# The last down unit of a mixture of experts, loaded and finished by column halves

## The chip, the cores and the metric

The kernel runs on one core of a Trainium2 chip. A time is the device time of one execution in microseconds (us), and the figure that counts is the median of several runs. A core has TensorE (matrix products; its weight loads are listed apart as PEld), VectorE (DVE), ScalarE (ACT), GpSimd (POOL) and SyncE (SP, which here only issues DMAs). Each engine works through its own queue in order; semaphores order the engines against each other. Numbers are 32-bit floats throughout.

## The reference

One layer of a decoder for 256 prompt rows and 32 sample rows of width 1024. Attention comes first and is not touched here. After it:

```python
logits = hx @ w_router + b_router            # 32 experts
top_val, top_idx = top_k(logits, 4)
comb = sum(one_hot(top_idx) * softmax(top_val))
for each expert e:
    gu   = hx @ w_gate_up[e] + b_gate_up[e]  # 1024 -> 2048
    gate = minimum(gu[:, 0::2], 7); up = clip(gu[:, 1::2], -7, 7)
    act  = gate * sigmoid(1.702 * gate) * (up + 1)
    acc += comb[:, e] * (act @ w_down[e] + b_down[e])   # 1024 -> 1024
out = layer_norm(alpha * hx + acc, ln2_g, ln2_b)
```

The weights of the 32 experts are 403 MB in all and are read once.

## The kernel before

The experts go in 16 pairs. Each expert computes only the rows that were routed to it: up to 64 rows in a first pass, gathered by products with a 0/1 matrix (`pick`). The two experts of a pair share TensorE: each product has 64 columns of the array, expert 0 in the upper and expert 1 in the lower 64 rows of the result. There are further passes for experts with more than 64 rows; they were not taken here (`further_passes` takes its `otherwise` branch).

The weights of a pair arrive in 12 units of 2 MB, in a ring of 9 slots of 16 KB a partition: units 0 to 7 are gate and up weights, units 8 to 11 down weights. SyncE issues all loads, in order, each as soon as its slot is free. The last pair has a routine of its own, `load_last_pair`. Its unit 11 comes in two loads of 1 MB, one for each of two contraction chunks `c`, each with its semaphore (`half_in[8 + c]`). When the gate and up products are done, SyncE loads the layer norm's gains and biases (`load_last`, semaphore `ln2_in`), behind the weights in the same queue.

On TensorE the end of the last pair is `last_down` and `mix_last`. `last_down` computes `y = act @ w_down` into two banks of 512 columns: bank 4 has the lower column half of `y`, bank 5 the upper. It runs over units `v` (8 to 11), chunks `c`, column halves and experts. Between, `keep_sums` copies the running sums of earlier pairs from `acc` into banks 0 to 3 and 7, by products with the identity, so that the last combine can add to them there: bank 2t + half has prompt tile `t`, and bank 7 the 32 sample rows, of which each quarter of 256 columns sits on 32 partitions (`mix_samples`, four products on 32 columns of the array each).

When both banks are done (`down_done`), ScalarE copies bank 4 to `ybuf` and VectorE copies bank 5 (`take_lower`, `take_upper`). `mix_last` waits for both and multiplies `ybuf` by `spread`, which holds the routing weights and puts the rows back in their places: tile 0, its two halves; the samples; tile 1, its two halves.

VectorE then takes the second layer norm. It first waits for `ln2_in`, and takes statistics from the banks (`y_statistics`, one `bn_stats` for each half, then `bn_aggr`): tile 0, the samples, tile 1. ScalarE takes the roots (`root_y`) and centres tile 0 out of the banks; VectorE multiplies tile 0 by the gain (GpSimd adds its bias), and does samples and tile 1 by itself. SyncE stores the pieces. A matrix product with a mean matrix (bank 6) joins the statistics of the four sample quarters.

Every product on 32-bit data appears in the trace as two passes, so that eight products of the source are sixteen in the trace.

Of the kernel before, what the change touches and what calls it, by code (L numbers as in the profile page):

```python
# [109 lines left out]
def build_layer(nc, x_prompt, x_sample, cache_k, cache_v, state_k, state_v, page_table, w_in, gn_moba,  # L110
# [9 lines left out]
    def place(name, shape, at=None, dt=F32):  # L120
# [89 lines left out]
    names = """ident_in consts_in x_in0 x_in1 x_in2 pages_in w_in_landed0 w_in_landed1 w_in_landed2 wout_in0 wout_in1  # L210
        wout_in2 wout_in3 k_landed0 k_landed1 k_landed2 k_landed3 v_landed0 v_landed1 v_landed2 v_landed3 ln1_in
        router_in bdn_in ln2_in x_turned xT_even xT_odd projected proj_copied kv_turned vtok_ready kstage_ready
# [12 lines left out]
        y_ready mixed added y_varied y_rooted y_scaled y_centred y_gained y_normed y_done y_moments y_shared  # L225
        sums_whole copies_out
        results_out dve_done dve_moe pass_added""".split()
# [4 lines left out]
    w_landed = [sems[f"w_in_landed{i}"] for i in range(3)]  # L232
    wout_in = [sems[f"wout_in{i}"] for i in range(4)]
    k_landed = [sems[f"k_landed{i}"] for i in range(KRING)]
# [167 lines left out]
    def _(sp):  # L402
# [107 lines left out]
        def load_last_pair():  # L510

            p, m = PAIRS - 1, PAIRS // PERIOD
            for u in range(8):
                unit_free(m, 0, u, WHOLE)
                dst = ring[slot_of(0, u)][:, :].rearrange("p (e k n) -> p e k n", e=2, k=2)
                k, c = 256 * (u % 4), slice(D * (u // 4), D * (u // 4) + D)
                for e in range(2):
                    sp.dma_start(dst[:, e], w_gate_up[0, 2 * p + e, k:k + 256, c].rearrange(
                        "(p k) n -> p k n", p=128)).then_inc(half_in[u], 16)
                sp.sem_inc(unit_in[slot_of(0, u)], 16)  # L520
            for u in range(8, UNITS - 1):
                unit_free(m, 0, u, WHOLE if u < RING else LATE)
                load_unit(p, 0, u)
            unit_free(m, 0, UNITS - 1, LATE)
            dst = ring[slot_of(0, UNITS - 1)][:, :].rearrange("p (e c n) -> p e c n", e=2, c=2)
            src = w_down[0, pair_of(p), 512:1024, :].rearrange("e (p c) n -> p e c n", c=4)
            for c in range(2):
                sp.dma_start(dst[:, :, c, :], src[:, :, 2 + c, :]).then_inc(half_in[8 + c], 16)
            sp.sem_inc(unit_in[slot_of(0, UNITS - 1)], 16)
# [205 lines left out]
    def _(pe):  # L735
# [341 lines left out]

        pe.wait_ge(wout_in[2], 16)
        pe.wait_ge(wout_in[3], 16)
        pe.wait_ge(S.outT_ready, 3)  # L1080
# [157 lines left out]

        def mix_samples(out, start):

            for q in range(4):
                ins = nc.tensor.matmul(out[NS * q:NS * q + NS, 0:256], spread[:, SEQ:T],
                                       ybuf[:, 256 * q:256 * q + 256], start=start, stop=True,
                                       tile_position=(0, NS * q))
            return ins
# [114 lines left out]
        def last_down():  # L1360
# [3 lines left out]
            keep_sums(2, 0)  # L1364
            for v in range(4):
                w = ring[slot_of(0, 8 + v)]
                if v < 3:
                    pe.wait_ge(unit_in[slot_of(0, 8 + v)], unit_value(last // PERIOD, 0, 8 + v))
                pe.wait_ge(S.actT_ready, last * 2 + (1 if v < 2 else 2))
                for c in range(2):  # L1370
                    j = 2 * v + c
                    if v == 3:
                        pe.wait_ge(half_in[8 + c], 16)
                    for half in range(2):
                        for e in range(2):
                            at = 2048 * e + 1024 * c + 512 * half
                            ins = nc.tensor.matmul(bank[4 + half][64 * e:64 * e + 64, :], actT[:, j, 64 * e:64 * e + 64],
                                                   w[:, at:at + 512], start=(j == 0), stop=(j == KC - 1))
                if v < 3:
                    ins.then_inc(S.unit_used, 1)  # L1380
                if v == 0:
                    turn_act(last, 2 * last + 2, (1,))
                    keep_sums(1, 0)
                if v == 1:
                    keep_sums(1, 1)
            ins.then_inc(S.down_done, 1)

# [7 lines left out]

        def mix_last():

            pe.wait_ge(S.y_ready, last * 2 + 2)
            for j in (0, 1, 4, 2, 3):
                t, half = divmod(j, 2)  # L1400
                if t == 2:
                    ins = mix_samples(bank[7], False)
                else:
                    ins = nc.tensor.matmul(bank[j][:, :], spread[:, 128 * t:128 * t + 128],
                                           ybuf[:, 512 * half:512 * half + 512], start=False, stop=True)
                ins.then_inc(S.mixed, 1)

        last_gate_up({1: lambda: combine(last - 1), 5: turn_first, 6: keep_first})
        last_down()
        mix_last()  # L1410

# [31 lines left out]
    def _(act):  # L1443
# [221 lines left out]

        def take_lower():
            act.wait_ge(S.down_done, PAIRS)
            copy(ybuf[:, 0:512], bank[4][:, :]).then_inc(S.y_ready, 1)

        nc.scalar.activation(s_(c_junk), s_(c_junk), ACT.Sqrt)  # L1670
        further_passes(act, more, none, first=take_lower, otherwise=take_lower)

# [15 lines left out]
    def _(dve):  # L1688
# [478 lines left out]

        def take_upper():
            dve.wait_ge(S.down_done, PAIRS)
            V.tensor_copy(ybuf[:, 512:1024], bank[5][:, :]).then_inc(S.y_ready, 1)  # L2170

        def sums_to_sbuf():
            take_upper()
            for n, j in enumerate((0, 1, 4, 2, 3)):
                t, half = divmod(j, 2)
# [7 lines left out]

        further_passes(dve, more, none, sums_to_sbuf, sums_kept, take_upper)
        dve.wait_ge(S.ln2_in, 160)
        mv = [s_(c_mv + 4 * t, 4) for t in range(3)]

        def y_statistics(t, after):
            for half in range(2):
                dve.wait_ge(S.mixed, 5 * last + after + half)  # L2190
                step.on(V.bn_stats(s_(c_stat + 12 * t + 6 * half, 6), bank[2 * t + half][:, :]))
            dve.wait_ge(step.sem, step.n)
            link(V.bn_aggr(mv[t][:, 0:2], s_(c_stat + 12 * t, 12).rearrange("p (a c) -> p a c", a=2)))
            V.tensor_scalar(mv[t][:, 1:2], mv[t][:, 1:2], LN_EPS, None, ALU.add).then_inc(S.y_varied, 1)

        y_statistics(0, 1)
        dve.wait_ge(S.mixed, 5 * last + 3)
        link(V.bn_stats(s_(c_stat + 24, 6), bank[7][:, 0:256]))
# [6 lines left out]
                               ALU.mult).then_inc(S.y_scaled, 1)  # L2205
        y_statistics(1, 4)
        dve.wait_ge(S.y_shared, 1)
# [4 lines left out]
        link(V.reciprocal(mv[1][:, 1:2], mv[1][:, 1:2]))  # L2212

        for half in range(2):
            c = slice(512 * half, 512 * half + 512)
# [42 lines left out]
```

## Time and profile before

| | us |
|---|---|
| median of three runs | 1143.01 |
| lowest, highest | 1141.0, 1143.07 |
| profiled execution, span from first to last instruction | 1138.4 |
| median less span (what lies around it) | 4.6 |
| TensorE busy in the span | 1100.8 |
| mean rate of all DMAs | 399 GB/s |

The profiled execution's time is its span, which leaves out what lies ahead of the first and behind the last instruction. The last gate and up products of the last pair end just before 1104 us, and the rest of the span holds what is described here. The granted clock of TensorE was 1.00 in all stretches between 1100 and 1130. DMA engines were at or over 0.99 busy until 1118 us and 0.53 in the us from 1120.

In rows, `PE` and `PEld` are TensorE's products and weight loads, `SPq` is SyncE issuing a DMA, and the bracket at a row's end is the idle time of the engine before it with what released it. Ends of TensorE's products are modelled.

### The profile page before, as it was taken

How to read it: one execution, taken by the hardware profiler on the slowest of the kernel's cores; microseconds unless marked ns; L12 is line 12 of the kernel's file. 1: busy time of each engine (PE TensorE's matmuls, PEld its weight loads, DVE VectorE, ACT ScalarE, POOL GpSimd, SP SyncE). 2: the span in 40 equal slices, each digit the busy share in tenths (PEclk: the TensorE clock that was granted, in tenths of full speed). 3: DMA queues.
4: the chain of work that ended last, by engine and by line, in shares of the span. 5: the costliest groups of instructions: out<-in, count | busy, mean ns of one | idle time of the engine just before them, and what ended most of it. 6: DMA issues, size and time to landing. Idle time of an engine off the chain costs nothing.

```text
span 1138.4 us, 14132 instructions
## 1 busy us (share of the span) xinstructions
PE 1100.8 (97%) x5468; PEld 462.9 (41%) x5469; DVE 293.2 (26%) x734; ACT 204.1 (18%) x481; POOL 30.2 (3%) x65
## 2 busy tenths in 40 slices
PE   8999999999999999999999999999999999999996
PEld 6876764433333333333333333333333333333331
DVE  1553757530303030212121212121202031303123
ACT  2322412411111120202020202020201111111112
POOL 0110111000000000000000000000000000000001
PEclk9999999999999999999999999999999999999998
DMA  9967778999999999999999999999999999999994
GB/s 361 347 221 247 286 274 344 418 431 408 429 420 425 432 431 430 430 430 431 432 429 431 432 431 432 431 431 431 431 431 432 432 431 431 431 430 430 397 423 192
DMA packets 61348, 454.37 MB, mean 399 GB/s; under 512 B 6595, under 2 KB 19539, under 8 KB 35572
## 3 DMA queue, kind: packets, MB, share of 16 engines
q1 hardware_dynamic: 58818, 440.97, 93.0%
q0 software_dynamic: 1728, 10.75, 2.5%
q10 hardware_dynamic: 754, 1.98, 0.4%
q8 instruction: 34, 0.56, 0.2%
q14 instruction: 14, 0.11, 0.0%
HBM read 450.14 MB, written 11.93 MB: 406 GB/s over the span
## 4 chain that ended last, share of the span: by engine, by line
PE 79%; DMA 16%; ACT 2%; DVE 1%; SPq 1%; issue 1%; DVEq 0%
PE bank L1176 26%; PE bank L1229 19%; DMA ring<-in_w_gate_up 15%; PE bank L737 6%; PE bank L764 6%; PE bank L1060 5%; PE bank L1256 3%; PE bank L1344 2%; PE bank L767 2%; PE bank L925 2%; PE bank L1056 1%; DMA ln_bs<-in_ln_b 1%; PE bank L882 1%; PE bank L1272 1%; ACT ybuf L1448 1%; ACT actT L1448 1%
## 5 line engine op out<-in xcount | busy, mean ns | idle before, releaser
L1176 PE MATMUL bank<-ring,xg 128*64 128x512 f32 x1904 | 417.6, 594 | 11.2 <-DMA ring<-in_w_gate_up 11.2
L1176 PEld LDWEIGHTS bank<-ring,xg 128*64 128x64 f32 x1904 | 137.6, 137 | 282.0 <-issue 279.8
L1229 PE MATMUL bank<-ring,actT 128*64 128x512 f32 x960 | 216.1, 597 | 4.1 <-ACT actT L1448 4.1
L2111 DVE TENSOR_TENSOR acc<-acc,bank 128x512 f32<-128x512 f32 x60 | 41.3, 688 | 484.8 <-PE bank L1256 484.7
L1602 ACT ACTIVATE sig<-gate 128x256 f32<-128x256 f32 x64 | 26.7, 417 | 526.0 <-DVE gate L2093 526.0
L1229 PEld LDWEIGHTS bank<-ring,actT 128*64 128x64 f32 x960 | 67.3, 137 | 119.9 <-issue 115.3
L2093 DVE TENSOR_SCALAR gate<-bank 128x256 f32<-128x256 f32 x64 | 26.9, 420 | 194.8 <-PE bank L1176 175.8
L764 PE MATMUL bank<-xT,wblk 128*128 128x288 f32 x256 | 65.4, 409 | 0.2 <-DVE xT L1701 0.2
L1593 ACT ACTIVATE xg<-bank,small 128x128 f32<-128x128 f32 x128 | 48.1, 457 | 97.0 <-PE bank L737 96.9
L1060 PE MATMUL bank<-hx,pick 128*128 128x512 f32 x128 | 59.2, 605 | 0.0
L1448 ACT ACTIVATE ybuf<-bank 128x512 f32<-128x512 f32 x63 | 36.0, 596 | 126.8 <-PE bank L1229 87.3
L1256 PE MATMUL bank<-ybuf,spread 128*128 128x512 f32 x120 | 58.4, 618 | 0.0
L764 PEld LDWEIGHTS bank<-xT,wblk 128*128 128x128 f32 x256 | 47.4, 190 | 14.6 <-issue 2.7
L1060 PEld LDWEIGHTS bank<-hx,pick 128*128 128x128 f32 x128 | 23.0, 189 | 34.3 <-issue 34.3
L1256 PEld LDWEIGHTS bank<-ybuf,spread 128*128 128x128 f32 x120 | 19.1, 188 | 39.0 <-DVE acc L2111 19.7
L925 PE MATMUL bank<-wout,outT 128*128 128x512 f32 x64 | 29.8, 603 | 0.0
L767 PE MATMUL bank<-wblk,xT 128*128 128x256 f32 x128 | 29.1, 380 | 0.0
L1344 PE MATMUL bank<-ring,xg 128*64 128x512 f32 x128 | 28.3, 595 | 0.0
L2097 DVE SCALAR_TENSOR_TENSOR up<-up,gate 128x256 f32<-128x256 f32 x64 | 27.2, 425 | 3.3
L737 PEld LDWEIGHTS bank<-keep,ybuf 128*128 128x128 f32 x128 | 17.7, 207 | 25.3 <-issue 24.3
L728 POOL TENSOR_TENSOR acc<-acc,ln_b_sb 128x512 f32<-128x512 f32 x2 | 3.0, 1502 | 941.5 <-DVE acc L2217 941.5
L2094 DVE TENSOR_SCALAR up<-bank 128x256 f32<-128x256 f32 x64 | 26.6, 415 | 0.0
(249 smaller groups left out, 707.5 us busy)
## 6 DMA issues: line engine op xcount, KB each, us to landing
ring<-in_w_gate_up SPq DMA_DIRECT2D x119, 2048.0 KB, 26.5
ring<-in_w_down SPq DMA_DIRECT2D x63, 2048.0 KB, 27.3
ring<-in_w_gate_up SPq DMA_DIRECT2D x16, 1024.0 KB, 20.1
wblk<-in_w_in SPq DMA_DIRECT2D x11, 1024.0 KB, 7.8
kring<-in_cache_k_moba SPq DMA_DIRECT2D x16, 256.0 KB, 7.3
vring<-in_cache_v_moba SPq DMA_DIRECT2D x16, 256.0 KB, 7.3
out<-in_state_k_win POOLq DMA_DIRECT2D x8, 512.0 KB, 5.0
out<-in_state_v_win POOLq DMA_DIRECT2D x8, 512.0 KB, 5.9
```

The source lines that it names most:

```text
L737: return nc.tensor.transpose(out, in_, ident[0:in_.shape[0], 0:in_.shape[0]])
L764: ins = nc.tensor.matmul(out[:, 0:T], w[:, k, 128 * c:128 * c + 128], xT[:, k, :], start=(k == 0), stop=(k == KC - 1))
L767: ins = nc.tensor.matmul(out[:, 0:256], xT[:, k, 128 * c:128 * c + 128], w[:, k, :], start=(k == 0), stop=(k == KC - 1))
L925: return nc.tensor.matmul(bank[2 * t + half][:, :], outT[:, k, t0:t0 + rows], wout[:, k, 512 * half:512 * half + 512], start=(k == 0), sto ...
L1060: return nc.tensor.matmul(bank[6 + a][:, :], pick[:, t, :], hx[:, t, 512 * a:512 * a + 512], start=False, stop=(t == 1))
L1176: ins = nc.tensor.matmul(bank[n][64 * e:64 * e + 64, :], xg[:, k, 64 * e:64 * e + 64], w[e][:, 512 * n:512 * n + 512], start=False, stop=( ...
L1229: ins = nc.tensor.matmul(bank[4 + half][64 * e:64 * e + 64, :], actT[:, j, 64 * e:64 * e + 64], w[e][:, at:at + 512], start=(j == 0), stop ...
L1256: ins = nc.tensor.matmul(bank[4 + half][:, :], spread[:, t0:t0 + rows], ybuf[:, 512 * half:512 * half + 512], start=True, stop=True)
L1344: ins = nc.tensor.matmul(bank[n][64 * e:64 * e + 64, :], xg[:, k, 64 * e:64 * e + 64], w[:, at:at + 512], start=False, stop=(k == KC - 1))
L1448: return nc.scalar.activation(out, in_, ACT.Copy, **kw)
L1593: ins = nc.scalar.activation(xg[:, k, :], turned, ACT.Identity, bias=s_(c_cols + KC + k), scale=s_(c_cols + k))
L2111: V.tensor_tensor(o, o, new, ALU.add).then_inc(S.added, 1)
```

## The change

Unit 11 is loaded by column halves instead of chunks: for each half, one load for each expert, of 512 KB in rows of 2 KB. On TensorE the products of unit 11 run half by half. Behind the lower half's come `mix_half(0)`, which waits for the copy of the lower half and combines it (both prompt tiles, two of four sample quarters), then the upper half's products and `mix_half(1)`. ScalarE does both copies (`take_halves`). VectorE takes the statistics of both tiles' lower halves first, then those of the upper halves and of the samples, which are now combined last; and it waits for gains and biases only before it uses them. A semaphore of the output projection's weights is merged with its neighbour, and `lower_done` is new.

```diff
-    wout_in = [sems[f"wout_in{i}"] for i in range(4)]
+    wout_in = [sems[f"wout_in{min(i, 2)}"] for i in range(4)]
...
-            dst = ring[slot_of(0, UNITS - 1)][:, :].rearrange("p (e c n) -> p e c n", e=2, c=2)
+            dst = ring[slot_of(0, UNITS - 1)][:, :].rearrange("p (e h c n) -> p e h c n", e=2, h=2, c=2)
             src = w_down[0, pair_of(p), 512:1024, :].rearrange("e (p c) n -> p e c n", c=4)
-            for c in range(2):
-                sp.dma_start(dst[:, :, c, :], src[:, :, 2 + c, :]).then_inc(half_in[8 + c], 16)
+            for h in range(2):
+                for e in range(2):
+                    sp.dma_start(dst[:, e, h], src[:, e, 2:4, 512 * h:512 * h + 512]).then_inc(half_in[8 + h], 16)
...
-        pe.wait_ge(wout_in[2], 16)
-        pe.wait_ge(wout_in[3], 16)
+        pe.wait_ge(wout_in[2], 32)
...
-        def mix_samples(out, start):
-
-            for q in range(4):
+        def mix_samples(out, start, quarters=range(4)):
+
+            for q in quarters:
...
-            for v in range(4):
+            for v in range(3):
                 w = ring[slot_of(0, 8 + v)]
-                if v < 3:
-                    pe.wait_ge(unit_in[slot_of(0, 8 + v)], unit_value(last // PERIOD, 0, 8 + v))
+                pe.wait_ge(unit_in[slot_of(0, 8 + v)], unit_value(last // PERIOD, 0, 8 + v))
                 pe.wait_ge(S.actT_ready, last * 2 + (1 if v < 2 else 2))
                 for c in range(2):
                     j = 2 * v + c
-                    if v == 3:
-                        pe.wait_ge(half_in[8 + c], 16)
                     for half in range(2):
                         for e in range(2):
                             at = 2048 * e + 1024 * c + 512 * half
                             ins = nc.tensor.matmul(bank[4 + half][64 * e:64 * e + 64, :], actT[:, j, 64 * e:64 * e + 64],
-                                                   w[:, at:at + 512], start=(j == 0), stop=(j == KC - 1))
-                if v < 3:
-                    ins.then_inc(S.unit_used, 1)
+                                                   w[:, at:at + 512], start=(j == 0), stop=False)
+                ins.then_inc(S.unit_used, 1)
                 if v == 0:
                     turn_act(last, 2 * last + 2, (1,))
                     keep_sums(1, 0)
                 if v == 1:
                     keep_sums(1, 1)
-            ins.then_inc(S.down_done, 1)
+            for half in range(2):
+                pe.wait_ge(half_in[8 + half], 32)
+                w = ring[slot_of(0, UNITS - 1)]
+                for c in range(2):
+                    for e in range(2):
+                        at = 2048 * e + 1024 * half + 512 * c
+                        ins = nc.tensor.matmul(bank[4 + half][64 * e:64 * e + 64, :], actT[:, 6 + c, 64 * e:64 * e + 64],
+                                               w[:, at:at + 512], start=False, stop=(c == 1))
+                ins.then_inc((S.lower_done, S.down_done)[half], 1)
+                mix_half(half)
...
-        def mix_last():
-
-            pe.wait_ge(S.y_ready, last * 2 + 2)
-            for j in (0, 1, 4, 2, 3):
-                t, half = divmod(j, 2)
-                if t == 2:
-                    ins = mix_samples(bank[7], False)
-                else:
-                    ins = nc.tensor.matmul(bank[j][:, :], spread[:, 128 * t:128 * t + 128],
-                                           ybuf[:, 512 * half:512 * half + 512], start=False, stop=True)
+        def mix_half(half):
+
+            pe.wait_ge(S.y_ready, last * 2 + half + 1)
+            for t in range(2):
+                nc.tensor.matmul(bank[2 * t + half][:, :], spread[:, 128 * t:128 * t + 128],
+                                 ybuf[:, 512 * half:512 * half + 512], start=False, stop=True).then_inc(S.mixed, 1)
+            ins = mix_samples(bank[7], False, (2 * half, 2 * half + 1))
+            if half:
                 ins.then_inc(S.mixed, 1)
 
         last_gate_up({1: lambda: combine(last - 1), 5: turn_first, 6: keep_first})
         last_down()
-        mix_last()
...
-        def take_lower():
-            act.wait_ge(S.down_done, PAIRS)
-            copy(ybuf[:, 0:512], bank[4][:, :]).then_inc(S.y_ready, 1)
+        def take_halves():
+            for half in range(2):
+                act.wait_ge(*((S.down_done, PAIRS) if half else (S.lower_done, 1)))
+                copy(ybuf[:, 512 * half:512 * half + 512], bank[4 + half][:, :]).then_inc(S.y_ready, 1)
 
         nc.scalar.activation(s_(c_junk), s_(c_junk), ACT.Sqrt)
-        further_passes(act, more, none, first=take_lower, otherwise=take_lower)
+        further_passes(act, more, none, first=take_halves, otherwise=take_halves)
...
-        def take_upper():
-            dve.wait_ge(S.down_done, PAIRS)
-            V.tensor_copy(ybuf[:, 512:1024], bank[5][:, :]).then_inc(S.y_ready, 1)
-
         def sums_to_sbuf():
-            take_upper()
-            for n, j in enumerate((0, 1, 4, 2, 3)):
+            for n, j in enumerate((0, 2, 1, 3, 4)):
...
-        further_passes(dve, more, none, sums_to_sbuf, sums_kept, take_upper)
-        dve.wait_ge(S.ln2_in, 160)
+        further_passes(dve, more, none, sums_to_sbuf, sums_kept)
         mv = [s_(c_mv + 4 * t, 4) for t in range(3)]
-
-        def y_statistics(t, after):
-            for half in range(2):
-                dve.wait_ge(S.mixed, 5 * last + after + half)
-                step.on(V.bn_stats(s_(c_stat + 12 * t + 6 * half, 6), bank[2 * t + half][:, :]))
-            dve.wait_ge(step.sem, step.n)
+        for t in range(2):
+            dve.wait_ge(S.mixed, 5 * last + t + 1)
+            link(V.bn_stats(s_(c_stat + 12 * t, 6), bank[2 * t][:, :]))
+
+        def y_statistics(t):
+            dve.wait_ge(S.mixed, 5 * last + t + 3)
+            link(V.bn_stats(s_(c_stat + 12 * t + 6, 6), bank[2 * t + 1][:, :]))
             link(V.bn_aggr(mv[t][:, 0:2], s_(c_stat + 12 * t, 12).rearrange("p (a c) -> p a c", a=2)))
             V.tensor_scalar(mv[t][:, 1:2], mv[t][:, 1:2], LN_EPS, None, ALU.add).then_inc(S.y_varied, 1)
 
-        y_statistics(0, 1)
-        dve.wait_ge(S.mixed, 5 * last + 3)
+        y_statistics(0)
+        dve.wait_ge(S.mixed, 5 * last + 5)
...
-        y_statistics(1, 4)
+        y_statistics(1)
...
+        dve.wait_ge(S.ln2_in, 160)
         for half in range(2):
```

## Rows read from the trace of the kernel before

**Rows 1.** Page of the profiled execution: span, busy us by engine.
```profile
span 1138.4 us, 14132 instructions
...
PE 1100.8 (97%) x5468; PEld 462.9 (41%) x5469; DVE 293.2 (26%) x734; ACT 204.1 (18%) x481; POOL 30.2 (3%) x65
```

**Rows 2.** Tail of the chain that ended last: start us, us, what.
```profile
1103.98 0.36 SPq L626
...
1112.54 12.15 DMA ln_bs<-in_ln_b
...
1129.78 1.29 DVE acc L2217 x2
```

**Rows 3.** Timeline of the tail, TensorE's part: start us, us, engine, line, operation.
```profile
1120.57 0.20 PEld L1377 LDWEIGHTS bank<-ring,actT 128*64 128x64 f32 x4 [0.95 <-DMA ring<-in_w_down]
...
1122.55 0.60 ACT L1448 ACTIVATE ybuf<-bank 128x512 f32<-128x512 f32 x1 [10.71 <-PE bank L1377]
1122.55 0.69 DVE L2170 COPY ybuf<-bank 128x512 f32<-128x512 f32 x1 [16.20 <-PE bank L1377]
...
1123.30 0.30 PEld L1404 LDWEIGHTS bank<-ybuf,spread 128*128 128x128 f32 x2 [1.68 <-DVE ybuf L2170]
...
1125.21 0.16 PEld L1242 LDWEIGHTS bank<-ybuf,spread 128*32 128x32 f32 x8 [0.76 <-issue]
1125.21 0.64 PE L1242 MATMUL bank<-ybuf,spread 128*32 128x256 f32 x8
1125.78 0.30 PEld L1404 LDWEIGHTS bank<-ybuf,spread 128*128 128x128 f32 x2 [0.41 <-issue]
```

**Rows 4.** Timeline of TensorE's matmuls alone, 1118.1 to 1122.6 us.
```profile
1117.75 4.75 PE L1377 MATMUL bank<-ring,actT 128*64 128x512 f32 x20
```

**Rows 5.** Line 1377, matmuls 1118.58 to 1119.0 us: ns min/median/max, first and last start.
```profile
L1377 PE MATMUL bank<-ring,actT x4: 592/592/592, 1118.2 to 1118.6; 128*64 128x512 f32 x4
```

**Rows 6.** Answer on line 528, the two loads of the last unit.
```profile
L528 SPq DMA_DIRECT2D ring<-in_w_down x2: 471/2988/5506, 1091.9 to 1092.4; - x2
...
DMA to landing us min/median/max: 25.5/26.8/28.1
```

**Rows 7.** Line 494, loads of the two units ahead of it.
```profile
L494 SPq DMA_DIRECT2D ring<-in_w_down x2: 2294/2294/2294, 1087.2 to 1089.6; - x2
...
DMA to landing us min/median/max: 22.9/24.1/25.4
```

**Rows 8.** DMA totals by stretch: 1085 to 1105 us, 4 KB rows prevailing.
```profile
DMA packets 1760, 8.48 MB, mean 424 GB/s; under 512 B 103, under 2 KB 103, under 8 KB 1347
```

**Rows 9.** DMA totals, 4 to 8 us, rows of 1 KB prevailing.
```profile
DMA packets 1014, 1.44 MB, mean 361 GB/s; under 512 B 66, under 2 KB 857, under 8 KB 1014
```

**Rows 10.** DMA issues of the whole run: KB each, median us to landing.
```profile
hx<-in_x_prompt SPq DMA_DIRECT2D x2, 512.0 KB, 4.6
```

**Rows 11.** Answer on line 1242 (sample products), 1125.20 to 1125.25 us.
```profile
L1242 PE MATMUL bank<-ybuf,spread x4: 403/403/403, 1125.2 to 1125.2; 128*32 128x256 f32 x4
```

**Rows 12.** Answer on line 1404 (combine products), 1123.5 to 1124.0 us.
```profile
L1404 PE MATMUL bank<-ybuf,spread x2: 593/645/697, 1123.3 to 1123.8; 128*128 128x512 f32 x2
```

**Rows 13.** Timeline of the tail, VectorE's and ScalarE's part.
```profile
1123.17 1.28 ACT L1675 ACT_TABLE_LOAD   x1
...
1124.71 1.31 DVE L2191 BATCH_NORM_STATS2 small<-bank 128x6 f32<-128x512 f32 x2 [1.46 <-DMA ln_bs<-in_ln_b]
...
1126.37 0.42 DVE L2198 BATCH_NORM_STATS2 small<-bank 128x6 f32<-128x256 f32 x1
...
1127.45 1.29 DVE L2191 BATCH_NORM_STATS2 small<-bank 128x6 f32<-128x512 f32 x2
1127.56 1.45 ACT L1681 ACTIVATE acc<-bank,small 128x512 f32<-128x512 f32 x2 [0.88 <-DVE small L2204]
...
1129.20 0.20 ACT L1675 ACTIVATE small<-small 128x1 f32<-128x1 f32 x1 [0.19 <-DVE small L2194]
...
1129.59 0.15 DVE L2212 RECIPROCAL small<-small 128x1 f32<-128x1 f32 x1
```

More of the change, by code:

```diff
@@ L210, in build_layer @@
     names = """ident_in consts_in x_in0 x_in1 x_in2 pages_in w_in_landed0 w_in_landed1 w_in_landed2 wout_in0 wout_in1
-        wout_in2 wout_in3 k_landed0 k_landed1 k_landed2 k_landed3 v_landed0 v_landed1 v_landed2 v_landed3 ln1_in
+        wout_in2 k_landed0 k_landed1 k_landed2 k_landed3 v_landed0 v_landed1 v_landed2 v_landed3 ln1_in
         router_in bdn_in ln2_in x_turned xT_even xT_odd projected proj_copied kv_turned vtok_ready kstage_ready
@@ L225, in build_layer @@
         y_ready mixed added y_varied y_rooted y_scaled y_centred y_gained y_normed y_done y_moments y_shared
-        sums_whole copies_out
+        sums_whole lower_done copies_out
         results_out dve_done dve_moe pass_added""".split()
```

## Prediction

> **What bounds the kernel now.** I read the page first. TensorE is busy 1100.8 of 1138.4 us [rows 1], so nothing at the end counts unless it changes when TensorE's last product ends, or what VectorE does after it. Then the chain of waits, from its end backwards: the last pieces are VectorE's second layer norm, with the loads of the gains and biases before them [rows 2]. The reader should distrust that load as a bound. It landed at 1112.54 + 12.15 = 1124.69. The first statistics started at 1124.71, and the two of them ran on to 1126.02 [rows 13]. But TensorE had the first combined half ready at about 1124.47 (second pass at 1123.84 + 0.59 [rows 12], and 0.04 for the release) and the second one, 0.86 later, at 1125.33. The second statistics began at about 1125.36 in any case. So the wait for the gains is hidden but for some 0.03 us.
>
> The timeline of the tail gives the true order: the last weights release TensorE at 1120.57, the two copies start at 1122.55 and end at 1123.15 and 1123.24, and the combine starts at 1123.30 [rows 3]. From 1124.71 VectorE has little rest until it scales the first tile at 1129.78 [rows 2, 13].
>
> The question for this change is how long TensorE idles for the last half-unit. TensorE's own row shows one run from 1117.75 to 1122.50 [rows 4]. Products go in pairs, one for each expert, at a step of 0.43 us, so that two steps lead to 1118.61, which [rows 5] show rounded; there unit 11 begins, right behind unit 10. Four more steps would have brought the second load's products to 1120.33, and they started at 1120.57. TensorE waited 0.24 us. That is all there is to be filled.
>
> **When the weights are there.** The two loads of the last unit were issued at 1091.9 and 1092.4 and took 25.5 and 28.1 us, so they landed at 1117.4 and 1120.5 [rows 6]. Unit 10, issued at 1089.6, took 25.4 and landed at 1115.0 [rows 7]. So 1 MB followed in 2.4 us, and the last in 3.1.
>
> **The loads, cut anew.** Two loads of 1 MB in rows of 4 KB become four of 512 KB in rows of 2 KB. No row shows 2 KB alone. Above lies the rate with 4 KB rows prevailing, 424 GB/s [rows 8]; below, that with 1 KB rows prevailing, 361 [rows 9]. One MB takes 2.47 or 2.90 us by these, so the lower half lands at 1117.4 to 1117.8. TensorE loads its first weights of that half one step ahead of the products, at 1118.18. The slack is 0.4 to 0.8 us, and I take the cost as nothing; without the cover it is at most 0.4. The upper half lands by 1121.4, and TensorE will not ask for it before 1123.67 (below). On SyncE's queue two more issues stand ahead of the gain loads. The two issues took 0.47 and 5.51 us, to 1097.9 [rows 6]; SyncE's next issue was at 1103.98 [rows 2]. Two more at 0.5 each cost nothing; at 5.5 each they end at 1108.9, and the gains land 4.9 later, at 1129.6. They are then wanted at 1132.0, because the change moves that wait behind the statistics. Cost: nothing at either bound.
>
> The Trainium skill (DMA: Bandwidth & Descriptors, section Bandwidth) speaks against the cut: it asks for DMAs of at least 1 MiB and gives a 1 MB transfer, issued by GpSimd there, 6.15 us (341 GB/s). By that figure, as an estimate, the lower half would land at 1121.2, 3.0 us late, and the time would be 1148.2. The trace does not agree for queued transfers, where 1 MB landed 2.4 us after what stood ahead [rows 6, 7].
>
> **TensorE's new order.** It is now: lower products, wait for the lower copy, lower combine, then the upper products. Queued behind that wait are all products of the upper half, with ScalarE's second copy behind them. Step by step:
> - Lower products: start 1118.61, as now. Three steps of 0.43, the last one's 0.59 [rows 5] and a release of 0.04 make 1.92: ScalarE copies at 1120.53. The copy takes 0.60 and TensorE follows 0.06 later (1123.24 to 1123.30) [rows 3]: 1121.19. TensorE has idled 0.7 us.
> - Lower combine: two tiles take 1.91 (1123.30 to 1125.21). Samples: four quarters now take 0.57 (1125.21 to 1125.78) [rows 3]. Two quarters are not shown. The four products of a pass start together, 403 ns each [rows 11], so half of them save no time: 0.57 again; by count it would be 0.29. I take 0.57, since the row shows them side by side. The upper products start at 1123.67, 3.10 us later than now.
> - Upper products: 1.98 as now (1120.57 to 1122.55): copy at 1125.65. ScalarE's 0.60 replaces VectorE's 0.69 and saves 0.09: TensorE at 1126.31. Combined: first tile after 1.17, at 1127.48; sample weights after 1.91, their products' end 0.64 later [rows 3], and a release: 1128.90.
>
> So the path to the combined second half is 2.15 us longer (1127.48 against 1125.33). The work was not hidden: it went in front of the upper products on the one engine that sets the end.
>
> **VectorE's saving, and where it goes.** Statistics of both lower halves are taken while TensorE works, 1.3 us in all. Of the first tile's, nothing was on the path. The second's, 0.65, was: two took 1.29 from 1127.45 [rows 13]. But sample statistics, which ran at 1126.37 without waiting, now wait for the samples' end at 1128.90: +2.53. With them moves the scale that ScalarE waits for. Its centring starts at 1127.56 + 2.53 = 1130.09 and takes 1.45 [rows 13]: 1131.54. VectorE has the second tile's variance at 1127.45 + 2.53 + 0.65 + 0.46 = 1131.09 (0.46 from the end of the two, 1128.74, to the root at 1129.20), ahead of that, so the 0.65 saved is mostly lost waiting: ScalarE's root runs 1131.58 to 1131.78, the reciprocal at 1131.81 instead of 1129.59. The scaling of tile 0 starts at 1132.00 instead of 1129.78 [rows 2, 13]. Sum: **+2.2 us**. From there nothing differs. The table load (1.28 us from 1123.17 [rows 13]) moves to 1126.28 and ends before the first root is wanted, at 1128.5. The merged semaphore of the output weights joins two adjacent waits: nothing.
>
> The profiled span is 1138.4; the median of the runs, 1143.01, has 4.6 around it that the change does not touch. Forecast: 1143.0 + 2.2 = **1145.2 us**. Its own range: with samples at 0.29 twice and their last products 0.28 shorter, +1.7; with releases and tile changes dearer by 0.1 at each of seven places, +2.9. So 1144.5 to 1145.9, allowing 0.2 at the low end for the copy. A measurement tells about 0.2% of this kernel, 2.3 us, from no change. The forecast lies on that edge.
>
> **Rivals.**
> - *The small loads come late.* A load of 512 KB alone took 4.6 us [rows 10]. If the lower half's two landed 4.6 after unit 10, at 1119.6, TensorE would start 1.4 late: +3.6, 1146.6. If all four came one behind the other, the upper half would land at 1133.4 and the time would be near 1155. For it: rows shorter than any in this stretch. Against it: the 2.4 us per MB behind a full queue [rows 6, 7]. 0.13 together, 0.02 of it for the second. The rule of the Trainium skill that is weighed above belongs here.
> - *The weights or gains come later than in this trace, on other executions: faster.* The place is the tail of the queue. Each us that the gains land after 1124.7 now costs one, and after the change nothing before 1132.0. Break-even is 2.2 us late; if the timed runs have them 4 us late, the change gains 1.8: 1141.2. Late upper weights alone cross over at 1122.8 and gain at most 0.9. For it: the gains landed within 0.1 us of being the bound. Against it: nothing shows them later. 0.10.
> - *No effect.* If the combine of the lower half fitted into TensorE's 0.24 us wait and the copy cost nothing, the 0.65 of statistics would come and go: 1143. Against it: 2.5 us of products do not fit. 0.05.
>
> **How the numbers follow.** The forecast has 0.72. Of it 0.32 lies over +2.3 and 0.40 below. Late loads add 0.13 to slower. Of late gains 0.04 are faster and 0.06 the same; no effect adds 0.05. So faster 0.04, same 0.51, slower 0.45. The range goes from 1142.6, which takes in no effect and small gains, to 1147.0, which takes in the first form of late loads.
>
> **What the profile after would show.** The lower copy at about 1120.5, its combine from 1121.2, the upper products starting without any wait for a DMA at 1123.7, 3 us after landing, the second copy at 1125.6, sample statistics waiting for TensorE, and tile 0 scaled near 1132. Lower products that wait for a DMA past 1118.6 would show late loads. Upper products released by a DMA would show that the weights, not the combine, set the end, and the sum would be wrong from that step on; so would upper products that start before the lower combine is done.

## The result, and the profile after

| | before | after |
|---|---|---|
| median of 14 runs, us | 1142.30 | 1144.66 |
| lowest, highest, us | 1139.74, 1143.07 | 1142.21, 1145.88 |
| profiled span, us | 1138.4 | 1142.4 |

The change made the kernel slower: 2.4 us by the medians, and a ratio of 1.0026 with a 95% interval of 1.0018 to 1.0033, which is 3.0 us with 2.1 to 3.8. The loss is small, but the interval leaves out 1. Forecast were 1145.2 us and a loss of 2.2 us. In the experiments below a few executions took far longer (1169 to 5176 us, the kernel before among them); medians, ratios and stretches leave them out.

The spans differ by 4.0 us, more than the medians. The timeline shows why, and why one span is a poor measure here. Read it from the first product of unit 11. These are rows of the timeline after, and they answer to [rows 3, 4, 5, 13].

```profile
1119.95 0.14 PEld L1388 LDWEIGHTS bank<-ring,actT 128*64 128x64 f32 x2 [0.28 <-issue]
1120.38 1.89 PE L1388 MATMUL bank<-ring,actT 128*64 128x512 f32 x8
...
1122.31 0.60 ACT L1450 ACTIVATE ybuf<-bank 128x512 f32<-128x512 f32 x1 [8.70 <-PE bank L1388]
1122.96 0.30 PEld L1405 LDWEIGHTS bank<-ybuf,spread 128*128 128x128 f32 x2 [1.58 <-ACT ybuf L1450]
...
1124.87 0.63 PE L1242 MATMUL bank<-ybuf,spread 128*32 128x256 f32 x4
...
1125.43 0.20 PEld L1388 LDWEIGHTS bank<-ring,actT 128*64 128x64 f32 x4 [0.41 <-issue]
...
1127.41 0.60 ACT L1450 ACTIVATE ybuf<-bank 128x512 f32<-128x512 f32 x1 [4.51 <-PE bank L1388]
...
1128.06 0.30 PEld L1405 LDWEIGHTS bank<-ybuf,spread 128*128 128x128 f32 x2 [1.58 <-ACT ybuf L1450]
...
1130.65 0.43 DVE L2196 BATCH_NORM_STATS2 small<-bank 128x6 f32<-128x256 f32 x1 [0.23 <-PE bank L1242]
...
1131.86 1.45 ACT L1684 ACTIVATE acc<-bank,small 128x512 f32<-128x512 f32 x2 [1.20 <-DVE small L2202]
...
1132.71 0.38 PE L1440 MATMUL bank<-small,keep 128*128 128x2 f32 x2 [2.11 <-issue]
1133.13 0.16 DVE L2206 COPY small<-bank 128x2 f32<-128x2 f32 x1 [0.27 <-PE bank L1440]
...
1133.65 0.15 DVE L2210 RECIPROCAL small<-small 128x1 f32<-128x1 f32 x1
...
1133.84 1.29 DVE L2216 TENSOR_TENSOR acc<-acc,ln_g_sb 128x512 f32<-128x512 f32 x2
```

Unit 11 begins at 1120.38 here and at 1118.61 before [rows 4, 5]. That 1.77 us arose ahead of everything that the change touches in TensorE's work. The executions of the kernels below that have no added delay began unit 11 anywhere between 1117.9 and 1121.5, kernels with the loads of before and of after among them, so it is scatter of the body. What the change does is the stretch from that first product to the scaling of tile 0: 1120.38 to 1133.84, **13.46 us**, against 1118.61 to 1129.78, **11.17 us** [rows 2]. It is 2.29 us longer.

In the rows the reader sees where. TensorE starts the lower combine at 1122.96 and the upper products at 1125.43. The bracket of that row names no DMA. The weight loads show the same 0.41 us in the kernel before, where they pass from the sample products to others at 1125.78 [rows 3]. The weights were there, as the answer on the line of the loads shows, for the first two issues (lower half) and then for the last two (upper half):

```profile
L529 SPq DMA_DIRECT2D ring<-in_w_down x2: 710/2988/5267, 1093.7 to 1094.4; - x2
...
DMA to landing us min/median/max: 22.2/23.6/25.0
```

```profile
L529 SPq DMA_DIRECT2D ring<-in_w_down x2: 4562/4574/4586, 1099.7 to 1104.4; - x2
...
DMA to landing us min/median/max: 18.0/18.3/18.7
```

The second issue, at 1094.4, took 25.0 us: the lower half was complete at 1119.4, before TensorE loaded the first of it at 1119.95. The last issue, at 1104.35, took 18.0 and landed at 1122.4. Its products started 3.0 us later.

### The profile page after: what moved, and what is told of

Read it like the earlier page. It is cut to its first block, busy times and chain, and to the rows that moved or that the text cites. A ratio compares the mean times of both kernels' runs of the same rounds, so it can differ in the third digit from the quotient of the medians.

```text
span 1142.4 us, 14134 instructions
## 1 busy us (share of the span) xinstructions
PE 1103.7 (97%) x5468; PEld 464.4 (41%) x5469; DVE 292.8 (26%) x733; ACT 204.6 (18%) x482; POOL 30.0 (3%) x65
## 3 DMA queue, kind: packets, MB, share of 16 engines
q10 hardware_dynamic: 754, 1.98, 0.4%
## 4 chain that ended last, share of the span: by engine, by line
PE 79%; DMA 17%; ACT 2%; DVE 1%; SPq 1%; issue 1%; DVEq 0%
PE bank L1176 26%; PE bank L1229 19%; DMA ring<-in_w_gate_up 16%; PE bank L738 6%; PE bank L765 6%; PE bank L1061 5%; PE bank L1256 3%; PE bank L768 2%; PE bank L926 2%; PE bank L1057 1%; PE bank L883 1%; ACT ybuf L1450 1%; PE bank L1374 1%; PE bank L1272 1%; ACT actT L1450 1%; PE bank L857 1%
```

## The experiments

All times are medians beside runs of the kernel before on the same chip, and the ratio is to those runs. The stretch is the one above, from unit 11's first product to the scaling of tile 0, in the profiled execution. In a kernel with the loop of before, that first product comes 3.48 us after the first of unit 10 (1115.13 to 1118.61 in the execution before), eight steps on.

| kernel | median, us | before beside it, us | ratio to before (95%) | stretch, us |
|---|---|---|---|---|
| before | 1142.30 | | 1 | 11.17 |
| after | 1144.66 | 1142.30 | 1.0026 (1.0018 to 1.0033) | 13.46 |
| after, again | 1143.51 | 1140.86 | 1.0016 (1.0007 to 1.0026) | 13.52 |
| early copy only | 1140.35 | 1140.86 | 0.9992 (0.9983 to 1.0000) | 10.01 |
| early copy only, again | 1140.75 | 1141.56 | 0.9995 (0.9986 to 1.0004) | 10.01 |
| samples last | 1143.15 | 1140.86 | 1.0017 (1.0007 to 1.0027) | 12.73 |
| gains' wait moved | 1141.82 | 1140.86 | 1.0005 (0.9996 to 1.0014) | 10.88 |
| before, delayed | 1148.60 | 1141.56 | 1.0066 (1.0052 to 1.0079) | 16.28 |
| after, delayed | 1143.76 | 1141.56 | 1.0025 (1.0014 to 1.0036) | 13.93 |
| after, delayed, again | 1143.86 | 1141.25 | 1.0029 (1.0019 to 1.0040) | 15.00 |
| early copy only, delayed | 1146.74 | 1141.56 | 1.0051 (1.0037 to 1.0065) | not read |
| early copy only, delayed, again | 1147.87 | 1141.25 | 1.0060 (1.0048 to 1.0072) | 16.37 |
| before, delayed, TensorE kept at work | 1144.98 | 1141.25 | 1.0038 (1.0025 to 1.0051) | 16.11 |

### The changed kernel again

> The changed kernel once more, beside the other three on one chip. Theory 1: from the first product of unit 11's lower half to the scaling of tile 0 it takes 13.4 to 13.5 us, where the kernel before took 11.2, whatever the time of the stages ahead; ratio to before 1.0020. Rival (something ahead of unit 11 became slower): that stretch is less than 13 us, and the difference lies ahead of it.

```profile
1119.49 1.89 PE L1388 MATMUL bank<-ring,actT 128*64 128x512 f32 x8
...
1133.01 1.29 DVE L2216 TENSOR_TENSOR acc<-acc,ln_g_sb 128x512 f32<-128x512 f32 x2
```

The stretch is 13.52 us, and unit 11 began 0.9 us earlier than in the first profile of this kernel. So the loss is in the stretch, and repeats to 0.06 us; nothing shows the stages ahead to be slower. By the ratio it is 1.8 us in this set, and was 3.0 in the first.

### The early copy alone

The loads, the order of unit 11's products, ScalarE's two copies and VectorE's late wait for the gains stay as changed. The combine goes behind both halves, in the order of before, and with it VectorE's statistics.

```diff
                 ins.then_inc((S.lower_done, S.down_done)[half], 1)
-                mix_half(half)
...
+            pe.wait_ge(S.y_ready, last * 2 + 1)
+            for n, j in enumerate((0, 1, 4, 2, 3)):
+                if n == 1:
+                    pe.wait_ge(S.y_ready, last * 2 + 2)
```

> As the changed kernel in its loads, the order of unit 11's products and ScalarE's two copies, but the whole combine stands behind both halves, in the order of the kernel before (tile 0, samples, tile 1). Theory 1 (the lower combine in front of the upper products is the loss): the upper products start right behind the lower ones, 1.9 us after them, and TensorE combines the lower half without a wait for a copy, 0.75 to 0.85 us earlier than the kernel before: 0.8 us faster than before (ratio 0.9993), 3.0 faster than the changed kernel. Rival 1 (the four small loads in 2 KB rows are the loss): the products of the upper half wait for a DMA, and the time stays 2 us or more above before. Rival 2 (two copies by ScalarE, one behind the other, are the loss): the second copy ends after 1.2 us and the time is 0.5 us above before.

```profile
1119.29 3.60 PE L1388 MATMUL bank<-ring,actT 128*64 128x512 f32 x16
...
1121.22 0.60 ACT L1454 ACTIVATE ybuf<-bank 128x512 f32<-128x512 f32 x1 [8.70 <-PE bank L1388]
...
1122.82 1.98 PE L1410 MATMUL bank<-ybuf,spread 128*128 128x512 f32 x4
1122.94 0.60 ACT L1454 ACTIVATE ybuf<-bank 128x512 f32<-128x512 f32 x1 [1.12 <-PE bank L1388]
...
1124.84 0.70 DVE L2191 BATCH_NORM_STATS2 small<-bank 128x6 f32<-128x512 f32 x1 [0.16 <-PE bank L1410]
...
1129.30 1.29 DVE L2218 TENSOR_TENSOR acc<-acc,ln_g_sb 128x512 f32<-128x512 f32 x2
```

Both halves' products are one run, 1119.29 to 1122.89. The lower copy ran beside the upper products, so TensorE starts to combine at 1122.82 without a wait. The second copy, 1122.94 to 1123.54, runs beside the first combined half. The stretch is 10.01 us: 3.45 less than after, and 1.16 less than before, of which 0.24 is the wait for weights that the execution before had. The other 0.92 is about the 0.8 that was expected. Rival 1 falls: the four small loads are in this kernel too, and cost nothing that shows. Rival 2 falls: so are the two copies by ScalarE.

> The kernel with the early copy and the combine behind both halves, once more, to tell whether its gain over before is one. Theory 1: 0.7 to 0.9 us faster (ratio 0.9993), and the stretch from the first product of unit 11 to the scaling of tile 0 takes 10.0 us, against 11.2 before, of which 0.24 was a wait for weights. Rival (chance): ratio at or above 1.0000.

```profile
1121.50 3.60 PE L1388 MATMUL bank<-ring,actT 128*64 128x512 f32 x16
...
1131.51 1.29 DVE L2218 TENSOR_TENSOR acc<-acc,ln_g_sb 128x512 f32<-128x512 f32 x2
```

The same stretch again, and a ratio whose interval includes 1. The traces show a gain of about 0.9 us in the stretch. By the ratios it is 0.6 to 0.9 us, at the edge of what the times can tell: one interval ends at 1.0000, the other goes beyond it. This is the best version found.

### The samples, all at the end

```diff
-            ins = mix_samples(bank[7], False, (2 * half, 2 * half + 1))
             if half:
-                ins.then_inc(S.mixed, 1)
+                mix_samples(bank[7], False).then_inc(S.mixed, 1)
```

> The changed kernel with all four sample quarters in the last combine. Theory 1, with two quarters as dear as four: the upper products start 0.57 us earlier after the lower combine's start than in the changed kernel, and the last sample product still takes 0.64: 0.57 us less than the changed kernel, 1.7 to 1.8 more than before (ratio 1.0015). Rival (two quarters cost half): what is saved ahead of the upper products, 0.29, is given back behind them, and the time is that of the changed kernel (1.0020).

```profile
1117.92 1.89 PE L1388 MATMUL bank<-ring,actT 128*64 128x512 f32 x8
...
1122.41 0.20 PEld L1388 LDWEIGHTS bank<-ring,actT 128*64 128x64 f32 x4 [0.76 <-issue]
...
1126.96 0.64 PE L1242 MATMUL bank<-ybuf,spread 128*32 128x256 f32 x8
...
1130.65 1.29 DVE L2215 TENSOR_TENSOR acc<-acc,ln_g_sb 128x512 f32<-128x512 f32 x2
```

The upper products start 4.49 us after the lower ones (1117.92 to 1122.41), in the changed kernel 5.05. So 0.56 us went, and at the end four quarters take hardly longer than two: VectorE's sample statistics start 2.62 us after the upper combine (1125.05 to 1127.67), and 2.59 in the changed kernel. Two quarters cost as much as four. In the changed kernel's own rows two quarters took 0.56 (1124.87 to 1125.43). The rival falls by the trace. The times don't tell: 1.0017 beside 1.0016 of the changed kernel on the same chip. The stretch fell by 0.73 against the first profile of the changed kernel, more than 0.56; the rest is that VectorE did not wait here for the product that joins the sample statistics (there 0.27).

### The gains' wait alone

```diff
-        dve.wait_ge(S.ln2_in, 160)
         mv = [s_(c_mv + 4 * t, 4) for t in range(3)]
...
+        dve.wait_ge(S.ln2_in, 160)
         for half in range(2):
             c = slice(512 * half, 512 * half + 512)
             dve.wait_ge(S.y_centred, half + 1)
```

> The kernel before with one edit: VectorE waits for gains and biases only before it uses them. Theory (that wait was hidden behind the combine of tile 0's upper half): statistics of the first half start up to 0.3 us earlier, those of the second do not, and the time is that of before within 0.05 us (ratio 1.0000). Rival (the gains usually land later than in the one trace): faster, by 0.5 us or more.

```profile
1115.73 7.09 PE L1377 MATMUL bank<-ring,actT 128*64 128x512 f32 x32
...
1124.77 0.70 DVE L2190 BATCH_NORM_STATS2 small<-bank 128x6 f32<-128x512 f32 x1 [1.22 <-PE bank L1404]
...
1125.63 0.70 DVE L2190 BATCH_NORM_STATS2 small<-bank 128x6 f32<-128x512 f32 x1 [0.16 <-PE bank L1404]
...
1130.09 1.29 DVE L2217 TENSOR_TENSOR acc<-acc,ln_g_sb 128x512 f32<-128x512 f32 x2
```

The first statistics start at 1124.77 as soon as their half is combined, and the second at 1125.63 wait for TensorE again (0.16 us). The stretch begins at 1115.73 + 3.48 = 1119.21 and takes 10.88: 0.29 less than before, nearly all of it the 0.24 us wait for weights that this execution didn't have. The interval of the ratio, 1.0005, includes 1. The wait was hidden.

### The upper half delayed

To see whether the change pays when the upper half is late, 2 MB of other weights are loaded between the two halves, into a slot that is free, in both kernels and in the one with the early copy. They are not used. One delay was tried, so from which lateness on the change pays was not measured.

```diff
+                if h == 0:
+                    unit_free(m, 0, UNITS, LATE)
+                    late = w_gate_up[0, pair_of(0), 0:256, :].rearrange("e (p c) n -> p e c n", c=2)[:, :, 0, :]
+                    sp.dma_start(ring[slot_of(0, 3)][:, :].rearrange("p (e n) -> p e n", e=2), late).then_inc(S.ln2_in, 16)
```

(In the kernel before, `c` stands for `h`. The waits for `ln2_in` count one load more.)

> The kernel before with 2 MB of other weights loaded between the two loads of unit 11, into a slot that is free by then; VectorE's wait for gains counts one load more. Theory 1: the second load lands 5.0 us later (2 MB at 420 GB/s), at about 1125.5, TensorE waits for it, and the whole tail moves by it: 4.9 us slower than before (ratio 1.0043). Rival (the end is set by something else than the last weights): clearly less than 4 us.

The kernel before with the delay, timeline and then windows (PEclk is the granted clock, 1.00 for 2.4 GHz and 0.50 for 1.2; columns as in the head row):

```profile
1117.41 5.37 PE L1381 MATMUL bank<-ring,actT 128*64 128x512 f32 x24
...
1126.53 3.38 PE L1381 MATMUL bank<-ring,actT 128*64 128x512 f32 x8 [3.75 <-DMA ring<-in_w_down]
...
1137.17 1.29 DVE L2221 TENSOR_TENSOR acc<-acc,ln_g_sb 128x512 f32<-128x512 f32 x2
```

```profile
core 0: us, PE busy (x) PEld busy (x) DVE busy (x) ACT busy (x) POOL busy (x), PEclk, DMA share, GB/s
...
1123.00:1124.00 1.00, 0.00 (x0) 0.00 (x0) 0.00 (x0) 0.00 (x0) 0.00 (x0) 1.00 1.05 414
...
1127.00:1128.00 1.00, 1.00 (x6) 0.26 (x4) 0.00 (x0) 0.00 (x0) 0.00 (x0) 0.50 0.44 150
...
1129.00:1130.00 1.00, 0.91 (x4) 0.00 (x0) 0.05 (x1) 0.06 (x1) 0.00 (x0) 0.50 0.04 12
...
1131.00:1132.00 1.00, 1.00 (x3) 0.38 (x2) 0.07 (x1) 0.84 (x1) 0.00 (x0) 1.00 0.00 0
```

TensorE idled 3.75 us for the second load. Then, at half the clock, the last eight products took 3.38 us; they take 1.94 to 1.98 at full clock. The stretch grew by 5.11: 3.68 us of later start (5.64 us after unit 11's first product, before 1.96) and 1.43 of clock. The second load was late as expected: issued at 1099.05 and 27.4 us on its way, it landed at 1126.4, 5.9 us later than before, of which 1.1 is a later start of unit 11's loads. But unit 11's products began at 1120.89, 2.3 us later than before, and so waited for less of it.

The expected 4.9 for the time was too little: the ratio says 7.5. The stretch accounts for 5.1 of it, and where the rest of the timed runs' loss lies is open. A longer time at the lower clock in some executions may be part of it. The two executions at 1147.6 us, one of them the profiled one, had a granted clock of 0.996 in the mean of the whole execution, and the three from 1148.6 to 1149.3 had 0.992 or 0.993. There is no trace of one of those three, so this is not shown, but the early-copy kernel with the delay (below) shows that the lower clock can last longer.

> The changed kernel with the same 2 MB between its lower and its upper half. Theory 1: lower copy and lower combine fit into the 5 us of waiting, of which the upper products lose only what lies behind the 3.1 us that the lower combine takes anyway: 1.8 us slower than the changed kernel, 4.0 slower than before (1.0035), so 0.9 faster than the kernel before with the same delay. The change pays when the upper half lands later than about 2.2 us after where it does. Rival (the lower combine costs its 2.2 us wherever it stands): 2 us or more above the kernel before with the same delay, 1.006.

```profile
1121.10 1.89 PE L1392 MATMUL bank<-ring,actT 128*64 128x512 f32 x8
...
1126.67 1.94 PE L1392 MATMUL bank<-ring,actT 128*64 128x512 f32 x8 [0.45 <-DMA ring<-in_w_down]
...
1135.03 1.29 DVE L2220 TENSOR_TENSOR acc<-acc,ln_g_sb 128x512 f32<-128x512 f32 x2
```

The same delay costs the changed kernel 0.47 us in the stretch: TensorE, busy with the lower combine, waited 0.45 us for the upper half. The products took 1.94 us. Here too unit 11 began late, at 1121.10, which makes the wait short.

> The changed kernel with the 2 MB between its halves, once more, beside the two others. Theory: the lower combine fills the wait, TensorE idles less than 1 us at a time, its clock stays at 1.00, and the stretch from unit 11's first product to the scaling of tile 0 takes 13.9 us; ratio 1.0025. Rival: the first run was a chance one and the ratio lies near that of the delayed kernel before, 1.005 or more.

```profile
1118.76 1.89 PE L1392 MATMUL bank<-ring,actT 128*64 128x512 f32 x8
...
1125.52 1.94 PE L1392 MATMUL bank<-ring,actT 128*64 128x512 f32 x8 [1.64 <-DMA ring<-in_w_down]
...
1133.76 1.29 DVE L2220 TENSOR_TENSOR acc<-acc,ln_g_sb 128x512 f32<-128x512 f32 x2
```

Here unit 11 began 2.3 us earlier, at 1118.76, and the wait for the upper half was 1.64 us. The clock stayed (products in 1.94 us), and the stretch was 15.00, not 13.9. The ratios, 1.0025 and 1.0029, are far from the 1.0066 of the delayed kernel before. With the delay the change is the faster by more than 4 us (4.2 to 4.7 by the ratios), not by the 0.9 expected.

> The kernel with early copy and the combine behind both halves, with the same 2 MB between the halves. Theory 1: only the early copy is hidden: 0.7 us less than the kernel before with the same delay, 4.2 above before (1.0037), so between the two others. Rival (early copies cost more when they run beside a waiting TensorE): at or above the kernel before with the same delay.

> The kernel with the early copy, the combine behind both halves and 2 MB between the halves, once more. Theory: TensorE idles as long as in the delayed kernel before, since nothing of the combine stands in the wait, and its clock falls too; it saves 0.7 to 1.0 us by the early copy, ratio 1.0055, stretch 15.3 to 15.6. Rival: the clock stays at 1.00 and the ratio is 1.0040 or less.

```profile
1121.78 1.89 PE L1392 MATMUL bank<-ring,actT 128*64 128x512 f32 x8
...
1126.94 3.68 PE L1392 MATMUL bank<-ring,actT 128*64 128x512 f32 x8 [3.28 <-DMA ring<-in_w_down]
...
1130.55 3.11 PE L1414 MATMUL bank<-ybuf,spread 128*128 128x512 f32 x4
...
1138.15 1.29 DVE L2222 TENSOR_TENSOR acc<-acc,ln_g_sb 128x512 f32<-128x512 f32 x2
```

With nothing to do in the wait, TensorE idled 3.28 us and took 3.68 for the eight products. The lower clock lasted longer than in the delayed kernel before, as one more window shows (columns as above):

```profile
1131.00:1132.00 1.00, 1.00 (x2) 0.39 (x2) 0.00 (x0) 0.98 (x2) 0.00 (x0) 0.50 0.00 0
```

It was 0.50 in every window from 1127 to 1132, and 1.00 again from 1133. So the first combine ran slowly too, 3.11 us for the four passes that take 1.98 at full clock. From the upper products' start to the sample products it took 6.65 us (1126.94 to 1133.59), against 3.72 in the kernel with the early copy and no delay: the clock cost 2.9 us here, and 1.4 in the delayed kernel before. That is why the stretch, expected at 15.3 to 15.6, was 16.37, and no shorter than the 16.28 of that kernel. The times, at 1.0051 and 1.0060, lie between those of the two others, as expected in order, but their intervals overlap that of the delayed kernel before, so a gain of the early copy with the delay is not shown. The first expectation's 1.0037 left the clock out.

### The delayed kernel before, with TensorE kept at work

```diff
+                    if v == 3 and c:
+                        for _ in range(4):
+                            nc.tensor.matmul(bank[6][:, :], ident, acc[:, 0, 0:512], start=True, stop=True)
```

The four products are of no use to the result.

> The kernel before with the 2 MB between its two loads, and with four products of the identity into bank 6, which nobody reads, while TensorE waits for the second load. In the delayed kernel TensorE idled 3.75 us, its granted clock then stood at 0.50, and the last eight products took 3.38 us instead of 1.93. Theory (part of that kernel's loss is the clock): the clock stays at 1.00, the eight products take 1.9 to 2.0, and the stretch from unit 11's first product to the scaling of tile 0 falls from 16.3 to 14.8; ratio to before 1.0052. Rival (the products are slow because their weights are only just there): they take 3.4 us again and the stretch stays at 16.3.

```profile
1117.44 5.37 PE L1384 MATMUL bank<-ring,actT 128*64 128x512 f32 x24
...
1122.74 3.70 PE L1378 MATMUL bank<-acc,keep 128*128 128x512 f32 x8
...
1127.82 1.94 PE L1384 MATMUL bank<-ring,actT 128*64 128x512 f32 x8 [1.38 <-DMA ring<-in_w_down]
...
1137.03 1.29 DVE L2224 TENSOR_TENSOR acc<-acc,ln_g_sb 128x512 f32<-128x512 f32 x2
```

The idle stretch before the last products shrank to 1.38 us and they took 1.94 us, so the clock is the cause of the slow products and the rival falls. The expected stretch of 14.8 was missed: the second load was issued 1.2 us later in this execution (1100.28 against 1099.05), with unit 11's start nearly the same, so that the products started 6.90 us after unit 11's first, against 5.64 without the four products. The time fell from 1.0066 to 1.0038. At full clock the delayed kernel before is thus at 1.0038, and the changed one at 1.0025 to 1.0029: 1.0 to 1.5 us for the overlap itself, where 0.9 was expected. The intervals overlap, so this part is not told from nothing; the more than 4 us for overlap and clock together is.

## Why the prediction was right

The forecast and its path held, step by step. Predicted and measured in the first profile after, in us:

| step | predicted | measured |
|---|---|---|
| lower products to lower copy | 1.92 | 1.93 |
| copy, and TensorE after it | 0.66 | 0.65 |
| lower combine, two tiles | 1.91 | 1.91 |
| two sample quarters | 0.57 | 0.56 |
| upper products to second copy | 1.98 | 1.98 |
| copy, and TensorE after it | 0.66 | 0.65 |
| upper combine to sample statistics | 2.59 | 2.59 |
| sample statistics to scaling of tile 0 | 3.10 | 3.19 |
| sum | 13.39 | 13.46 |

- *The loss is TensorE's order.* The early-copy kernel differs from the changed one in where the lower combine, with its two sample quarters, stands and in the statistics that follow it, and the stretch fell by 3.45 us. It has the changed kernel's loads, product order and copies.
- *The loads cost nothing.* The lower half landed at 1119.4, 2.7 us after unit 10 (issued at 1091.32, it took 25.4 us), between the 2.47 and 2.90 that were worked out. SyncE's issues were near the dear bound: 0.71, 5.27, 4.59 and 4.56 us, and its next issue came at 1110.33 instead of 1103.98, of which 1.8 us is the scatter of the body (the first of these loads was issued 1.8 us later). As predicted, nothing waited for it. The 4.6 us of [rows 10], which the prediction gives to a load by itself, is the median of two loads issued one behind the other at the kernel's start, with others behind them; the first rival, which was priced by it, did not happen.
- *The rule of at least 1 MiB a DMA* (the Trainium skill, DMA: Bandwidth & Descriptors, section Bandwidth) did not decide here. Its figure, as an estimate, would have had the lower half 6.15 us behind unit 10; it landed 2.7 us behind it.
- *Two quarters cost as much as four.* Shown by the rows (0.56 and 0.57 us) and by the kernel with the samples last.
- *VectorE's saved statistics are lost waiting.* The second tile's variance was ready before ScalarE had centred tile 0, as predicted. One wait was not foreseen: VectorE's copy of the joined sample statistics waited 0.27 us for TensorE's product, which started 1.14 us after the moments (each quarter's mean and mean square) were ready instead of the 0.84 before. Where there was no such wait, in the kernel with the samples last and in the second trace of the changed kernel with the delay, the same step took 2.98 and 3.02 us. So the 3.10 was 0.1 too long, and the wait took that back and 0.09 more.
- *Late weights.* The mechanism of this rival was right, and its size was not: the term "at most 0.9" left out that TensorE's clock fell to 0.50 in the wait. With the lower combine in the wait the products of the upper half took 1.94 us, at full clock, in both traces. In the kernel as it stands the upper half lands 3.0 us too early for any of this, so the rival did not happen.
- *No effect* needed a lower combine that fits into 0.24 us. It took 3.1 with its copy.
- *What was luck.* The time of 1145.2 began from 1143.0, the median of three runs, and took the 4.6 us between that and the span as lying around the span. In every timed run the time is only 1.8 to 2.0 us above the span (1144.25 and 1142.4 for the profiled execution after). So, as an estimate from the span, the profiled execution before took about 1140.2 us, nearly 3 us less than that median, and most of the 4.6 is scatter between executions. This did not touch the forecast difference. That difference started from an execution with 0.24 us of waiting for weights; against the 10.88 of an execution without it the changed kernel loses 2.6 us. The times, 3.0 us in one set and 1.8 in the other, don't tell 2.2 from 2.6, and lie on both sides of the 2.3 us that the prediction gave as the edge between slower and the same.

## What to carry to other kernels

Work that is moved into a wait for weights must be measured against that wait on the engine that will carry it. Here TensorE waited 0.24 us and was given 3.1 us to do ahead of the last products. The copy, on an idle engine, could move early at no price; the combine could not. With 2 MB more ahead of the last weights the wait was there, and the same order of work was the faster one by more than 4 us. Most of that went when TensorE was kept at work with useless products, so most of it is the clock. Before a combine is cut into halves, look also at its narrow products, which may cost the same at half the number.

## What was not expected

- After 3.75 us without a product TensorE's granted clock went from 1.00 to 0.50 and was 1.00 again in the window from 1131. After 3.28 us it went to 0.50 too, and was 1.00 again only from 1133, though the products had begun only 0.4 us later. So the shorter idle stretch had the longer time at the lower clock; why was not tried. After idle stretches of 1.64 and 1.38 us it stayed at 1.00 in these runs, as the products' 1.94 us show.
- SyncE took 4.6 to 5.5 us for one issue of 512 KB while earlier loads were on their way, and 0.5 to 0.7 for the first of the four (traces of the changed kernel and of the one with the early copy).
- The joining product of the sample statistics started 1.14 us after VectorE had the moments in the changed kernel (the 2.11 us in its row begin at TensorE's last other product, 0.97 before the moments were ready), and 0.84 us after them in the kernel before. In the other traces it is 0.35 to 1.35 us, and the longest is in the first profile of the kernel with the early copy, which has the order of work of before. So the order doesn't explain it. It cost VectorE 0.27 us in the changed kernel, and the cause stays open.
